# Opening of a two-block transformer kernel: constants laid out by the host, two modulation chunks multiplied on the matmul engine, and the window bias formed there from float32 steps

## The reference, cut to what matters

```
cond = silu(c)
for l in range(2):                                   # first block
    mod = cond @ w_mod[l] + b_mod[l]                 # 1024 x 9216: nine chunks of 1024
    sh1, sc1, g1, sh2, sc2, g2, sh3, sc3, g3 = split(mod, 9)
    h = rms_norm(x, norm_g[l, 0]) * (1 + sc1) + sh1  # needs chunks 0 and 1
    x = x + 0.5 * g1 * swiglu(h, w_ffn1_gu[l], w_ffn1_down[l])
    h = rms_norm(x, norm_g[l, 1]) * (1 + sc2) + sh2
    proj = h @ w_in[l]                               # three attentions follow
    # window attention: scores + bias, masked to the last 128 keys
    bias = rel_table[t5_bucket(pos_q - pos_k)]       # 32 buckets x 6 heads, the same in both layers
    x = x + g2 * (mix @ w_out[l])
    x = x + 0.5 * g3 * swiglu(modulate(x), w_ffn2_gu[l], w_ffn2_down[l])
# second block: two layers of mod2, attention without softmax, swiglu; then a last rms norm
```

## Time and profile before

| | us |
|---|---|
| median of 3 runs (lowest, highest) | 1988.02 (1985.91, 1989.9) |
| the profiled execution | 1989.94 |
| its span, first to last instruction | 1988.1 |
| PE busy in the span | 1830.0 (92%) |
| DVE busy | 1402.3 (71%) |
| ACT busy | 932.5 (47%) |
| mean granted TensorE clock | 0.975 |

### The profile page before, as it was taken

One profiled execution on the slowest core, in us unless ns is written; L12 is line 12 of the kernel. 1 busy time (PEld: TensorE's weight loads), 2 busy tenths in 40 slices (PEclk: granted clock), 3 DMA queues, 4 the chain that ended last, 5 costly groups with the idle time before them and its releaser, 6 DMA issues.

```text
span 1988.1 us, 24161 instructions
## 1 busy us (share of the span) xinstructions
PE 1830.0 (92%) x9068; PEld 1485.3 (75%) x9068; DVE 1402.3 (71%) x1942; ACT 932.5 (47%) x1480; POOL 153.5 (8%) x280
## 2 busy tenths in 40 slices
PE   1699986789999999978999999999999999999997
PEld 0577865678887888767788877877878788877886
DVE  5668787568787788775778775567787765577554
ACT  1443353764446444657544454436344544445443
POOL 1011100101110111001011000000111000000000
PEclk9999998889999999998999999999999999999999
DMA  6789834049886998431689756354898564447552
GB/s 230 255 286 361 314 102 137 22 149 328 306 310 208 318 319 317 133 125 43 240 311 329 262 207 211 115 188 163 318 352 290 180 220 135 167 148 275 196 185 85
DMA packets 242298, 439.48 MB, mean 221 GB/s; under 512 B 16200, under 2 KB 156550, under 8 KB 241926
## 3 DMA queue, kind: packets, MB, share of 16 engines
q1 hardware_dynamic: 204810, 304.75, 45.3%
q0 software_dynamic: 36320, 131.13, 17.4%
q10 hardware_dynamic: 1052, 2.06, 0.3%
HBM read 436.79 MB, written 1.09 MB: 220 GB/s over the span
## 4 chain that ended last, share of the span: by engine, by line
PE 73%; DVE 13%; DMA 6%; ACT 5%; issue 3%; SPq 0%; DVEq 0%; ACTq 0%
PE bank L1597 22%; PE bank L1598 21%; PE bank L1599 21%; DVE weights_lo L979 4%; DMA arena<-in_w_mod 2%; DMA arena<-in_w_ada 2%; PE bank L1760 1%; DVE mod_acc L1003 1%; DVE arena L1096 1%; DMA weights_raw<-in_w_ffn_gu 1%; DVE x L1160 1%; ACT weights_hi L568 1%; DVE arena L1154 1%; DMA weights_raw<-in_w_ffn_in 1%; DVE hT_lo L1105 1%
## 5 line engine op out<-in xcount | busy, mean ns | idle before, releaser
L979 DVE TENSOR_TENSOR weights_lo<-weights_raw,weights_hi 128x1024 fp32r<-128x1024 f32 (+2 forms) x584 | 673.0, 1201 | 175.4 <-ACT weights_hi L568 175.1
L1597 PE MATMUL bank<-weights_hi,hT_hi 128*128 128x512 f32 x1760 | 699.8, 398 | 31.9 <-DVE hT_lo L1105 20.7
L1599 PE MATMUL bank<-weights_hi,hT_lo 128*128 128x512 f32 x1760 | 686.9, 390 | 0.0
L1598 PE MATMUL bank<-weights_lo,hT_hi 128*128 128x512 f32 x1760 | 686.6, 390 | 0.0
L568 ACT ACTIVATE weights_hi<-weights_raw 128x1024 fp32r<-128x1024 f32 (+2 forms) x584 | 572.0, 1037 | 143.2 <-PE bank L1599 86.1
L1597 PEld LDWEIGHTS bank<-weights_hi,hT_hi 128*128 128x128 f32 x1760 | 333.5, 189 | 115.4 <-issue 28.5
L1599 PEld LDWEIGHTS bank<-weights_hi,hT_lo 128*128 128x128 f32 x1760 | 333.0, 189 | 68.9
L1598 PEld LDWEIGHTS bank<-weights_lo,hT_hi 128*128 128x128 f32 x1760 | 334.0, 190 | 63.4
L1003 DVE SCALAR_TENSOR_TENSOR mod_acc<-arena,silu_cond,mod_acc 128x1024 f32<-128x1024 f32 x198 | 254.1, 1284 | 59.7 <-DMA arena<-in_w_mod 26.4
L711 ACT ACTIVATE actT_hi<-bank 128x512 fp32r<-128x512 f32 x66 | 39.6, 599 | 490.1 <-PE bank L1760 490.1
L1597 PE MATMUL bank<-weights_hi,actT_hi 128*128 128x512 f32 (+1 forms) x544 | 215.0, 395 | 6.2 <-DVE weights_lo L979 6.2
(11 more groups left out here) (275 smaller groups left out, 1288.5 us busy)
## 6 DMA issues: line engine op xcount, KB each, us to landing
weights_raw<-in_w_ffn_gu SPq DMA_DIRECT2D x176, 512.0 KB, 5.5
arena<-in_w_mod POOLq DMA_DIRECT2D x144, 512.0 KB, 6.7
weights_raw<-in_w_in SPq DMA_DIRECT2D x112, 512.0 KB, 4.6
arena<-in_w_ada POOLq DMA_DIRECT2D x96, 512.0 KB, 6.3
weights_raw<-in_w_ffn_down SPq DMA_DIRECT2D x88, 512.0 KB, 4.9
weights_raw<-in_w_ffn_in SPq DMA_DIRECT2D x88, 512.0 KB, 5.4
weights_raw<-in_w_ffn_out SPq DMA_DIRECT2D x44, 512.0 KB, 4.6
weights_raw<-in_w_out SPq DMA_DIRECT2D x32, 512.0 KB, 4.4
```

Of the source, the lines that this page charges most:

```text
L979: V.tensor_tensor(wlo[:, slot, 0:width], raw[:, slot, 0:width], whi[:, slot, 0:width].bitcast(F32), ALU.subtract).then_inc(S("lo_done"), 1)
L1597: T.matmul(o, sh, wh, start=start, stop=False)
L1598: T.matmul(o, sh, wl, start=False, stop=False)
L1599: return T.matmul(o, sl, wh, start=False, stop=stop)
```

## The change

The vectors come as one laid-out tensor (`vectors`, already columns), and positions, `rel_bias`, thresholds and rope frequencies as one (`pairs`); both are copied and repeated on the host. The constant tile is loaded in two parts, 544 columns at once and 1536 after the first phase's x is split. SP issues these two, then the 16 first modulation units and, with no wait, the first weights. Both chunks are multiplied wholly on PE (`mod_unit` of PE), between them the six bias passes, now with one float32 step each. DVE builds `reached` in two float32 buffers and takes a result out with mask and factor in one instruction. The rope angles go to POOL, their sine into the third strip of the first `ffn`; POOL's modulation loads start after `hi_done` 10. The first phase splits its weight units between the groups of x. The `mid1` code has no bias left.

```
-            load_rows(sp, 0, 6)
-            sp.dma_start(con[:, :], A["con"]).then_inc(S("const_loaded"), 16)
-            sp.dma_start(x[:, :, :], A["x"][0].rearrange("(t p) n -> p t n", p=P)).then_inc(S("x_loaded"), 16)
...
-            sp.wait_ge(S("mod_used"), 12)
...
+            sp.dma_start(vec[:, :], A["vectors"]).then_inc(S("vec_loaded"), 16)
+            sp.dma_start(ar(A_BIAS, B_END), A["pairs"]).then_inc(S("pos_loaded"), 16)
+            for m in range(MOD_FIRST_UNITS):
+                mod_load(sp, m)
...
+        def mod_load(eng, m):
+            name, layer, col = mod_source(m // 8)
+            k, was = m % 8, m - MOD_RING
+            if 0 <= was < MOD_FIRST_UNITS and was % 8 < 7:
+                eng.wait_ge(S("mod_read"), was - was // 8 + 1)
+            elif was >= 0 and on_pe(was):
+                eng.wait_ge(S("mod_summed"), was // 8 + 1)
...
-            for m in range(8 * MOD_CHUNKS[0][0]):
-                mod_load(m)
+            angles()
+            pool.wait_ge(S("hi_done"), RING + PREFETCH)
...
-            load_rows(act, 6, 13)
-            act.wait_ge(S("vec_ready"), 1)
+            act.dma_start(con[:, 0:C_FIRST], A["con"][:, 0:C_FIRST]).then_inc(S("const_loaded"), 16)
+            act.dma_start(x[:, :, :], A["x"][0].rearrange("(t p) n -> p t n", p=P)).then_inc(S("x_loaded"), 16)
+            act.wait_ge(S("vec_loaded"), 16)
...
+            def bias_reach(q):
+                need(dve, S("bias_summed"), q - 1)
+                q0, kb, c0 = (0, P, P)[q // 2], (0, 0, 1)[q // 2], 16 * (q % 2)
+                V.tensor_tensor(reached[q % 2], posf_q[:, q0:q0 + P].unsqueeze(1).broadcast_to([P, 16, P]),
+                                posf_k[:, kb, c0:c0 + 16].unsqueeze(2).broadcast_to([P, 16, P]), ALU.is_ge).then_inc(S("reached"), 1)
+            def bias_take(q):
+                dve.wait_ge(S("bias_summed"), q + 1)
+                for g in range(4):
+                    c = P * (q // 2) + 32 * g + 16 * (q % 2)
+                    ins = V.scalar_tensor_tensor(bias[:, :, c:c + 16], bank[4 + g][:, 0:96].rearrange("p (k h) -> p h k", h=WH), HD ** 0.5,
+                                                 con[:, C_MASKW + c:C_MASKW + c + 16].unsqueeze(1).broadcast_to([P, WH, 16]), ALU.mult, ALU.add)
+                ins.then_inc(S("bias_taken"), 1)
...
+            def mod_unit(m):
+                chunk, k = m // 8, m % 8
+                mod_wait(pe, m)
+                parts = modw[:, m % MOD_RING, :].rearrange("p (k r j) -> p r k j", r=4, j=32)
+                for r in range(4):
+                    ins = T.matmul(bank[sum_bank(chunk)][32 * r:32 * (r + 1), 0:256], silc[:, k:k + 1].broadcast_to([P, 32]), parts[:, r],
+                                   start=k == 0, stop=k == 7)
+                ins.then_inc(S("mod_summed" if k == 7 else "mod_read"), 1)
...
-                        ins = T.matmul(bank[4 + g][:, 3 * WH * k:3 * WH * (k + 1)], reached[r, k, :], bparts[r].rearrange("p q h -> p (q h)"),
-                                       start=True, stop=True)
+                        ins = T.matmul(bank[4 + g][:, WH * k:WH * (k + 1)], reached[q % 2][r, k, :], bstep[r, :], start=True, stop=True)
...
+BIAS_AFTER = (2, 4, 6, 8, 11, 13)
+X_TURN_AFTER = 9
...
+                    for u in range(MOD_FIRST_UNITS):
+                        mod_unit(u)
+                        if u in BIAS_AFTER:
+                            bias_pass(BIAS_AFTER.index(u))
+                        if u == X_TURN_AFTER:
+                            pe.wait_ge(S("const_loaded"), 16)
+                            x_turn(0, TRX_FIRST)
+                    pe.wait_ge(S("bias_taken"), 6)
+                    x_turn(1, TRX_FIRST)
+                    keep_warm(WARM[0])
                     first_strip(n0, strip_banks, None)
+                    pe.wait_ge(S("const_loaded"), 32)
```

More of the change, by code:

```diff
@@ L75, in on_pe @@
 def on_pe(m):
-    c0, c1 = next(c for c in [(0, 2)] + MOD_CHUNKS if 8 * c[0] <= m < 8 * c[1])
+    if m < MOD_FIRST_UNITS:
+        return True
+    c0, c1 = next(c for c in MOD_CHUNKS if 8 * c[0] <= m < 8 * c[1])
     return m % 8 == 7 and c1 - c0 > 5
@@ L380, in build, with mod_sem, mod_wait @@
         latent_hi, latent_lo = [ahi[:, 0], kvhi], [alo[:, 0], kvlo]
[L382 to L402, removed]
+        def mod_load(eng, m):
[5 more added lines that the diff above has]
+                eng.wait_ge(S("mod_summed"), was // 8 + 1)
+            else:
+                need(eng, S("mod_used"), taken(was + 1))
+            eng.dma_start(modw[:, m % MOD_RING, :], A[name][layer][k * P:(k + 1) * P, col:col + D]).then_inc(S(mod_sem(m)), 16)
+        def mod_sem(m):
+            return f"first_mod_loaded{m % MOD_RING}" if m < MOD_FIRST_UNITS else f"mod_loaded{m % MOD_RING}"
+        def mod_wait(eng, m):
+            loads = m // MOD_RING + 1
+            eng.wait_ge(S(mod_sem(m)), 16 * (loads if m < MOD_FIRST_UNITS else loads - MOD_FIRST_UNITS // MOD_RING))
         block = ctx.enter_context(nc.Block())
@@ L1251, in _ @@
             mod_store(0)
-            mod_units(range(8, 16))
-            for u in range(PREFETCH):
-                lo_static(RING + u, SLOT)
+            bias_reach(4)
+            bias_take(3)
+            bias_reach(5)
+            bias_take(4)
+            bias_take(5)
             mod_store(1)
@@ L1638, in last_rows @@
                 ins.then_inc(S("mm_done"), 2)
-            pe.wait_ge(S("const_loaded"), 16)
-            pe.wait_ge(S("rows_loaded"), 13 * 16)
-            for t in range(3):
-                r = P if t < 2 else V_ROWS2
-                T.transpose(bank[t][:, 0:r], rows[0:r, t, :], ident[0:r, 0:r]).then_inc(S("vecT_ready"), 1)
             def mod_sum(chunk):
@@ L2049 @@
     con, con2 = constants()
-    for name, a in [(k, inputs[k]) for k in INPUTS] + [("con", con), ("con2", con2)]:
+    laid = {k: inputs[k] for k in INPUTS if k not in ("positions", "rel_bias") and k not in [name for _, name in VECTORS]}
+    laid["vectors"], laid["pairs"] = vector_columns(inputs), pair_columns(inputs)
+    for name, a in list(laid.items()) + [("con", con), ("con2", con2)]:
         a = np.ascontiguousarray(a)
```

274 lines of the change are left out of this document (139 added, 135 removed).

## The result

| us | before | after |
|---|---|---|
| median (lowest, highest; 4 runs each) | 1988.30 (1985.91, 1989.90) | 1974.81 (1972.68, 1976.91) |
| the profiled execution | 1989.94 | 1976.91 |

The ratio is 0.9933, 95% interval 0.9916 to 0.9950: 13.5 us faster, where 42 were forecast, and outside the range. The two profiled executions differ by 13.03 us, and the traces say where that comes from.

The account below looks back on a forecast made before the run. PE was busy 92% of the span, so time could be won where it stands still or runs slow. 1989.94 - 23.8 - 20.3 + 1.5 = 1947.3, less 1.9: 1945.5, stated as 1946 us; range 1939 to 1970.

Parts of the forecast that it names:

- Term 1: First mid1: without the bias it takes what the second mid1 takes for the same piece; -23.8 us.
- Term 2: Opening: the first strip ends at 61.3 instead of 81.6 us; -20.3 us.
- (a): Opening, first data: modulation unit 2 is there at about 11.5 us and read at 12.4.
- (b): Opening: sixteen modulation units on PE take 7 us at the fast clock, 14 at the slow.
- (f): Opening behind the last pass: scale at 44.7 us, first product at 47.7, first strip ends at 61.3.
- (e): Opening: rounds of two units and a pass take 4.7 us each; pass 5 ends at 42.3.
- (c): Opening: a float32 bias pass, four row groups at a time, takes 3.5 us fast or 6.8 slow.
- the third rival: Opening: two row groups at a time, not four; a pass of 7.0 us, +19, 1965 us; chance 0.08.
- 64 loads in a row: Bias pass, worked out from the skill page's program order: 7.0 us per pass instead of 3.5, 1965 us.
- (d): Opening: PE runs at the fast clock from the middle of pass 0 on; pass 0 costs 5.2 us.
- Rival 2: Clock stays low through the opening: pass 6.8 us, opening ends at about 85, 1969 us; chance 0.22.
- Term 3: Behind the first strip: PE waits for the rest of the constants; +1.5 us, bounds 0 and 3.

Follow-up runs that it names:

- experiment 1: The kernel before the change with the relative bias left out of the first mid1; 1964.07 us, ratio 0.9875.
- experiment 9: The changed kernel with twenty products of zeros on PE while it waits for the first modulation tile, six moving columns kept; 1970.02 us, ratio 0.9900.
- 3: The changed kernel with PE's wait for the second part of the constants moved to the first sum that reads them; 1976.96 us, ratio 0.9937.
- 5: The changed kernel with thirty moving columns instead of six in each float32 product of the passes; 1973.24 us, ratio 0.9920.
- 6: The changed kernel with two full products of zeros ahead of each bias pass; 1979.69 us, ratio 0.9945.
- 10: The changed kernel with twenty products of zeros at the start and thirty moving columns in the passes; 1971.40 us, ratio 0.9909.
- 12: The changed kernel with twenty-six products of zeros at the start and thirty moving columns in the passes; 1970.23 us, ratio 0.9907.
- experiment 13: The changed kernel with each pass folded into 16 float32 products of all 128 rows and 24 moving columns; 1972.67 us, ratio 0.9909.
- 14: Changed kernel with 16 full-row products a pass, constants' wait moved, twelve zero products before the first strip, three modulation tiles in one strip; 1966.96 us.
- 7: The kernel of experiment 4 with PE's wait for the second part of the constants moved to the first sum that reads them; 1945.45 us, ratio 0.9785.
- experiment 4: The changed kernel with the passes in three bfloat16 parts, 18 moving columns, still in the opening; 1944.27 us, ratio 0.9776.

## Why the prediction was wrong

**Term 1, the twin.** Right: -23.8 forecast, -24.0 measured alone (experiment 1), 23.9 between the traces. A second instance of the same code without the suspect work was worth more than any sum over instructions.

**Term 2, (a), (b), (f).** Right at the level that the clock had: unit 2 read at 12.6 (12.4 forecast), sixteen units took 15.9 us (14 was the slow bound), the tail 19.7 us for 19.0. Some sums in the working don't come out: (e) adds up to 42.1 and not 42.3, the scale in (f) to 44.4 and not 44.7, and four steps of 1.6 us don't make the 13.6 us of the first strip, which took 13.4; that figure was lucky. None of it matters beside 21 us.

**Term 2, (c), the pass side by side.** Right, but it needs care: 7.01 us is both four row groups at a time at the low level (6.8) and two at a time, or one load after the other, at the fast one (7.0, the third rival). The units beside it decide: 1.94 for two is the low level, where one load after the other would have made 14 us. And at the fast level passes took 3.75 to 3.95, which the forecast's 3.5 and no other rival gives. The Trainium skill, "TensorE: Matmul & The Clock Gate", Step-by-step: what each phase is for, has matmuls in program order. By the prediction's working that makes 64 loads in a row, 7.0 us; the 3.75 us of pass 0 in experiment 9 are half of it and do not agree.

**Term 2, (d), "I take the fast level from the middle of pass 0 on".** This is the step that failed. I read from the earlier trace rows that PE speeds up when it works without a break, but those rows were products of 512 moving columns. Here PE is busy without a break from 11.5 to 68.7, and five of six passes, with the units around them, ran at 1.2 GHz (7.01 us a pass, 1.94 for two units; the granted clock is 0.50 from 60 to 65). So 39.0 us of passes stand where the forecast had 22.7.

Why the level was low is open. Of the nine traces with float32 passes (the changed kernel, 3, 5, 6, 9, 10, 12 to 14), the level rose by pass 4, behind the eight turns of x, in seven and not in two (experiments 3 and 13), with the same program ahead of it in the changed kernel and in 3; passes 1 to 3 were at the low level in all nine. Neither thirty moving columns (5, 10, 12), nor two full products ahead of a pass (6), nor a fast start (9, 12), nor full rows (13) kept the passes fast. What it is in these products was argued in the expectations and is not shown.

Rival 2 had the mechanism and nearly the size: opening end about 85 for 83.1, 1969 us, 0.22. Its chance was too small because I counted on a busy PE being a fast one. The rows at hand on short moving operands were at both levels, 387.44 to 387.67 at the fast and 397.93 to 398.84 at the low one, and could not decide it.

**Term 3, behind the first strip.** Forecast +1.5, bounds 0 and 3; in the trace +6.0 in the second strip. The wait itself, 2.88, was inside the bounds; that PE comes back at the low level and pays it a second time was left out. But removing it gave nothing (experiments 3 and 7), because weights and modulation tiles are late in the same strips: weight slots come free later in the new order. SP issues the eleventh weight tile at 83.65, after the end of the first strip, where the kernel before did so at 76.90, 4.7 us ahead of it. The forecast let those units "come just in time". The term was mis-sized, and for another reason than the trace's releaser names.

**The range.** 1974.8 lies 5 us above its end. Rival 2 alone, at 1969, would have been inside; with term 3 at its real size it is 1973.5.

**The larger question** was not asked in the forecast: whether float32 was needed at all. Moving the bias under the loads was right; changing its form at the same time cost 30.5 us of the 44 that the change gives with the bfloat16 form (experiment 4).

## What to carry to other kernels

With few moving columns, price a product from a record of the same weight type and column count at the low clock level (here 6, 24 and 30 columns cost the same), and take the fast level only where rows with the same kind of product are fast. When work is moved into a hole of PE, move it in its cheapest form; three bfloat16 parts beat one float32 product tenfold here. When removing a wait gives nothing, follow what is queued in order behind the next late tile on the helper engines: edits that gave nothing came with 3 us less once that tile was taken a strip later.

## What the hardware showed that I had not expected

- A pass of 64 bfloat16 products (32 rows, 128 weight columns, 18 moving columns) took 0.67 us with low-level units on both sides (experiment 4) and 0.64 in the fast stretch of the earlier trace rows: its 0.010 us a product didn't follow the clock. The float32 one took 7.01 and 3.75, 0.109 and 0.059 a product. The Trainium skill, "TensorE: Matmul & The Clock Gate", Weight-path perf modes, has a faster weight load for 128 columns of a type other than float32; the sign agrees. An estimate from the factor of about 2 that this page gives as measured, and from the two records of a float32 product, is four times; the rows have ten at the low level and six at the fast one.
- In these traces the granted clock reads 1.00 ahead of its first change, whatever the level: in experiment 13 it read 1.00 for the whole opening while every pass took 7.02 or 7.03 us. Here the level of an opening has to be read from the length of records.
- Thirty moving columns cost what six cost: 7.05 and 7.01 us for 128 records at the low level, 3.77 and 3.75 at the fast one.
